# Rows of normalised v scaled during the last gate, output tiles held back for two norm waits, and two more weight slots in conv back

## The reference

```
for layer, mixer in ((0, pool), (1, conv), (2, sgu), (3, pool)):
    h = rmsnorm(x, g);  [branch..., z] = h @ W_in
    x = x + (mixer(branch) * silu(z)) @ W_out
sgu: vn = layernorm(v, ng, nb);  s = tril(W_s) @ vn + b   (chunks of 128 positions, 4 heads);  y = u * s
outputs: rmsnorm(x), pooling and conv histories,
         new_sgu_prompt = vn of the prompt's last 128 frames, new_sgu_sample = vn of the sample frames
```

## Time and profile before

| | us |
|---|---|
| three runs: lowest, median, highest | 3535.90, 3884.73, 4079.17 |
| the profiled execution | 3532.74 |
| its span on the slowest core (core 2) | 3531.3 |
| spans of the eight cores | 3508.8, 3529.5, 3531.3, 3507.0, 3502.7, 3525.1, 3499.4, 3521.7 |
| busy on core 2: PE, DVE, ACT, POOL | 3398.8, 2626.1, 1422.9, 759.2 |
| mean granted TensorE clock of core 2, share of full speed | 0.989 |

### The profile page before, as it was taken

One profiled execution on the slowest core, in us unless ns is written; L12 is line 12 of the kernel. 1 busy time (PEld: TensorE's weight loads), 2 busy tenths in 40 slices (PEclk: granted clock), 3 DMA queues, 4 the chain that ended last, 5 costly groups with the idle time before them and its releaser, 6 DMA issues.

```text
span 3531.3 us, 58242 instructions; the slowest of 8 cores (3499.4 to 3531.3 us)
## 1 busy us (share of the span) xinstructions
PE 3398.8 (96%) x17839; PEld 1709.5 (48%) x18112; DVE 2626.1 (74%) x4357; ACT 1422.9 (40%) x2202; POOL 759.2 (21%) x1388
## 2 busy tenths in 40 slices
PE   7999999999999999899999999999999899999997
PEld 3444444554555554444554444444455444444554
DVE  6879998986778877998765554555555788888886
ACT  3334443434455555655542333333233233333332
POOL 2323333312343342000011111111111221111220
PEclk9999999999999999999999999999999999999999
DMA  7798888578866668987886655774457843333343
GB/s 138 175 229 182 196 176 196 160 231 170 155 137 143 139 148 273 288 273 226 257 255 203 188 144 179 211 218 133 158 184 207 279 149 114 114 105 105 103 153 109
DMA packets 393329, 635.89 MB, mean 180 GB/s; under 512 B 170728, under 2 KB 234728, under 8 KB 385728
## 3 DMA queue, kind: packets, MB, share of 16 engines
q0 software_dynamic: 74960, 308.29, 34.3%
q1 hardware_dynamic: 318064, 323.86, 31.0%
HBM read 561.12 MB, written 197.23 MB: 215 GB/s over the span
## 4 chain that ended last, share of the span: by engine, by line
PE 85%; DMA 4%; DVE 4%; issue 3%; ACT 2%; SPq 1%; POOL 0%; DVEq 0%; ACTq 0%; POOLq 0%
PE ps L661 52%; PE ps L799 24%; PE ps L1502 6%; DMA arena<-xin 2%; PE ps L1233 1%; DVE arena L749 1%; DMA arena<-yd 1%; PE ps L861 1%; PE ps L1573 1%; DMA arena<-wq 1%; SPq L704 1%; DVE arena L742 0%; DMA arena<-wst 0%; DVE arena L958 0%; PE ps L1023 0%
## 5 line engine op out<-in xcount | busy, mean ns | idle before, releaser
L661 PE MATMUL ps<-arena 128*128 128x512 bf16 (+1 forms) x10195 | 2136.6, 363 | 24.3 <-DVE arena L958 4.8
L661 PEld LDWEIGHTS ps<-arena 128*128 128x128 bf16 x10368 | 1006.3, 98 | 1007.2 <-issue 33.6
L799 PE MATMUL ps<-arena 128*128 128x512 bf16 (+1 forms) x4546 | 951.6, 362 | 15.9 <-DVE arena L1412 5.7
L799 PEld LDWEIGHTS ps<-arena 128*128 128x128 bf16 x4608 | 450.6, 98 | 480.1 <-issue 21.8
L618 POOL DMA_DIRECT2D arena<-wq x435 | 231.3, 532 | 1398.3 <-PE ps L799 676.8
L958 DVE TENSOR_TENSOR arena<-arena 128x526 f32<-128x526 f32 (+6 forms) x720 | 472.5, 661 | 59.8 <-ACT arena L938 26.7
L712 ACT ACTIVATE arena<-arena 128x512 bf16<-128x512 f32 (+1 forms) x360 | 211.4, 591 | 647.8 <-DVE arena L803 601.4
L803 DVE TENSOR_TENSOR arena<-ps,arena 128x512 f32<-128x512 f32 (+1 forms) x288 | 184.4, 641 | 136.5 <-PE ps L799 120.7
L724 DVE TENSOR_TENSOR arena<-arena 128x512 f32<-128x512 bf16 (+3 forms) x258 | 165.6, 642 | 122.0 <-ACT arena L712 121.7
L979 ACT ACTIVATE arena<-ps 128x512 f32<-128x512 f32 (+1 forms) x288 | 161.7, 561 | 214.2 <-PE ps L661 206.0
L938 ACT ACTIVATE arena<-ps 128x512 f32<-128x512 f32 (+2 forms) x288 | 157.4, 547 | 207.8 <-PE ps L661 163.3
(11 more groups left out here) (97 smaller groups left out, 2543.6 us busy)
## 6 DMA issues: line engine op xcount, KB each, us to landing
arena<-wq POOLq DMA_DIRECT2D x435, 512.0 KB, 5.7
wq<-wst POOLq DMA_DIRECT2D x88, 512.0 KB, 8.0
xs<-arena SPq DMA_DIRECT2D x144, 256.0 KB, 7.0
arena<-xs SPq DMA_DIRECT2D x144, 256.0 KB, 6.7
arena<-wst POOLq DMA_DIRECT2D x64, 512.0 KB, 8.3
arena<-hd SPq DMA_DIRECT2D x26, 1024.0 KB, 7.8
arena<-xin SPq DMA_DIRECT2D x96, 256.0 KB, 7.9
yd<-arena SPq DMA_DIRECT2D x96, 256.0 KB, 5.4
```

Source lines behind the costliest of these rows:

```text
L661: r = e.matmul(P[:, 0:T], lhsT=W[:, k * 256 + base:k * 256 + base + 128], rhs=H[:, k * st:k * st + T], start=(k == 0), stop=(k == 7))
L799: r = e.matmul(P[:, 0:T], lhsT=W[:, k * 128:(k + 1) * 128], rhs=ym[k].ap(BF16)[:, 0:T], start=(k == 0), stop=(k == 15))
```

## The change

- `sgu_norm` no longer scales and stores the rows. It notes the chunk's f32 tile, its statistics and its output in `self.rows_out`.
- `row_steps` makes ten steps of it: for each quarter of the columns one tile with both parameter rows (ng and nb, one load of 512 KB, placed in pool vn), used by both chunks: three VectorE operations for each quarter and chunk (subtract-and-scale of 512 columns, multiply, add); then two stores. One step is written after each gate tile of group 8, from the third on.
- Pulls in the gating layer: group 0 pulls after quarters 1, 3, 5, 7, 9 and 12 of its 16 (counted from 0), the last group five times over its 12, and `pull(2)` after the last norm is `pull(3)`.
- Stage C may use two more slots, at R+116 KB and R+48 KB, and its CAP is 11. Its ym tiles of groups 1 to 8 are kept to 28 places, the upper of which end at R+48 KB.

```diff
-        self.slots = Pool(S, "slot", 4096, slots + A_ex + D_ex + C_ex + [R + 43 * kb, b + 45 * kb])
-        self.SL = {... "C": list(range(8)) + [26, 27, 28, 29], ...}
+        self.slots = Pool(S, "slot", 4096, slots + A_ex + D_ex + C_ex + [R + 43 * kb, b + 45 * kb] + [R + 116 * kb, R + 48 * kb])
+        self.SL = {... "C": list(range(8)) + [26, 27, 28, 29, 32, 33], ...}
-        self.CAP = {"A": 17, "B": 1, "C": 9, "D": 11, "E": 17}
+        self.CAP = {"A": 17, "B": 1, "C": 11, "D": 11, "E": 17}
...
-        o = self.ymp.tile(list(range(16 if g == 0 else 32)))
+        o = self.ymp.tile(list(range(16 if g == 0 else 28)))
...
-                    if (it % 2 == 1 if g == 0 else 6 * (it + 1) // (4 * nch) > 6 * it // (4 * nch)):
+                    if (it in (1, 3, 5, 7, 9, 12) if g == 0 else (5 if g == MIX else 6) * (it + 1) // (4 * nch) > (5 if g == MIX else 6) * it // (4 * nch)):
                         self.pull()
...
-            self.pull(2)
+            self.pull(3)
             hn = self.load_h(g + 1) if g + 1 < NG else None
             ym = []
+            steps = self.row_steps() if g == MIX else []
             for ct in range(16):
...
                 self.sgu_gate(g, ct, h, vns, bt, ym)
+                if steps and ct > 1:
+                    steps.pop(0)()
...
         if keep or samp:
-            S.add("dve", ... tensor_scalar of all 2048 columns ...)
+            self.rows_out.append((vr, sm, 1 if samp else 0))
+        return vn
+
+    def row_steps(self):
...
+        def step(q, vr, sm, t):
+            c = slice(q * 512, (q + 1) * 512)
+            if t.no not in loaded:
+                loaded.add(t.no)
+                src = self.sgrow[:, :, c].rearrange("i p c -> p i c")
+                S.add("sp", lambda e: e.dma_start(out=t.ap().rearrange("p (i c) -> p i c", i=2), in_=src), writes=[t], cost=0.45,
+                      nbytes=128 * 4096, dk=t)
+            S.add("dve", ... tensor_scalar(out=vr.ap()[:, c], ... op0=ALU.subtract, op1=ALU.mult) ...)
             for i, op in ((0, ALU.mult), (1, ALU.add)):
-                for q in range(4):
-                    t = self.tp.tile()
-                    S.add("sp", ... dma_start(out=t.ap(), in_=self.sgrow[i, :, q * 512:(q + 1) * 512]) ...)
-                    S.add("dve", ... tensor_tensor of quarter q ...)
-            S.add("sp", ... dma_start(out=dst, in_=vr.ap()) ...)
+                S.add("dve", ... tensor_tensor(out=vr.ap()[:, c], ..., in1=t.ap()[:, i * 512:(i + 1) * 512], op=op) ...)
...
+        for q in range(4):
+            t = self.vn.tile()
+            for vr, sm, i in self.rows_out:
+                out.append(lambda q=q, vr=vr, sm=sm, t=t: step(q, vr, sm, t))
+        for vr, sm, i in self.rows_out:
+            out.append(lambda vr=vr, i=i: store(vr, i))
+        return out
```

More of the change, by code:

```diff
@@ L527, in layout @@
         D_ex = offs(R + 102 * kb, 4096, 2) + offs(R + 38 * kb, 4096, 4)
-        self.slots = Pool(S, "slot", 4096, slots + A_ex + D_ex + C_ex + [R + 43 * kb, b + 45 * kb])
-        self.SL = {"A": list(range(20)), "B": [30, 31, 6, 7], "C": list(range(8)) + [26, 27, 28, 29], "D": list(range(8)) + [20, 21, 22, 23, 24, 25]}
+        self.slots = Pool(S, "slot", 4096, slots + A_ex + D_ex + C_ex + [R + 43 * kb, b + 45 * kb] + [R + 116 * kb, R + 48 * kb])
+        self.SL = {"A": list(range(20)), "B": [30, 31, 6, 7], "C": list(range(8)) + [26, 27, 28, 29, 32, 33], "D": list(range(8)) + [20, 21, 22, 23, 24, 25]}
         self.SL["E"] = self.SL["A"]
-        self.CAP = {"A": 17, "B": 1, "C": 9, "D": 11, "E": 17}
+        self.CAP = {"A": 17, "B": 1, "C": 11, "D": 11, "E": 17}
         self.zs = Pool(S, "zs", 2048, zs + C_zs + offs(R + 36 * kb, 2048, 8) + offs(R, 2048, 10))
@@ L1487, in sgu_layer @@
         h = self.h_next
+        self.rows_out = []
         for i, g in enumerate(range(NG)):
@@ L1544, in sgu_norm @@
         if keep or samp:
-            S.add("dve", lambda e: e.tensor_scalar(out=vr.ap(), in0=vr.ap(), scalar1=sm.ap()[:, 24:25], scalar2=sm.ap()[:, 27:28],
-                                                   op0=ALU.subtract, op1=ALU.mult),
-                  reads=[(sm, "r"), (sm, "mv")] + [(vr, q) for q in range(4)], writes=[(vr, q) for q in range(4)], cost=c_stt(2048))
-            for i, op in ((0, ALU.mult), (1, ALU.add)):
-                for q in range(4):
-                    t = self.tp.tile()
-                    src = self.sgrow[i, :, q * 512:(q + 1) * 512]
-                    S.add("sp", lambda e, t=t, src=src: e.dma_start(out=t.ap(), in_=src), writes=[t], cost=0.45, nbytes=128 * 2048, dk=t)
-                    S.add("dve", lambda e, t=t, q=q, op=op: e.tensor_tensor(
-                        out=vr.ap()[:, q * 512:(q + 1) * 512], in0=vr.ap()[:, q * 512:(q + 1) * 512], in1=t.ap(), op=op),
-                        reads=[t, (vr, q)], writes=[(vr, q)], cost=c_tt(512))
@@ L1556, in sgu_norm, with store @@
-            dst = self.o_sgu[1 if samp else 0]
-            S.add("sp", lambda e: e.dma_start(out=dst, in_=vr.ap()), reads=[(vr, q) for q in range(4)], writes=[("o_sgu", samp)],
-                  cost=0.45, nbytes=128 * 8192, dk=vr)
-        return vn
+            self.rows_out.append((vr, sm, 1 if samp else 0))
+        return vn
+    def row_steps(self):
+        S = self.S
+        out = []
+        def step(q, vr, sm, t):
[5 more added lines that the diff above has]
+                      nbytes=128 * 4096, dk=t)
+            S.add("dve", lambda e: e.tensor_scalar(out=vr.ap()[:, c], in0=vr.ap()[:, c], scalar1=sm.ap()[:, 24:25],
+                                                   scalar2=sm.ap()[:, 27:28], op0=ALU.subtract, op1=ALU.mult),
+                  reads=[(sm, "r"), (sm, "mv"), (vr, q)], writes=[(vr, q)], cost=0.41)
+            for i, op in ((0, ALU.mult), (1, ALU.add)):
+                S.add("dve", lambda e, i=i, op=op: e.tensor_tensor(out=vr.ap()[:, c], in0=vr.ap()[:, c],
+                                                                   in1=t.ap()[:, i * 512:(i + 1) * 512], op=op),
+                      reads=[t, (vr, q)], writes=[(vr, q)], cost=c_tt(512))
+        def store(vr, i):
+            S.add("sp", lambda e: e.dma_start(out=self.o_sgu[i], in_=vr.ap()), reads=[(vr, q) for q in range(4)],
+                  writes=[("o_sgu", i)], cost=0.45, nbytes=128 * 8192, dk=vr)
+        loaded = set()
+        for q in range(4):
[5 more added lines that the diff above has]
+        return out
```

## The result

The kernel after ran at 3509.23, 3512.24 and 3513.08 us, and once at 3989.87. Executions in which the cores of a die ran at a visibly lower clock, such as the last, are left out of every ratio here. The ratio to the kernel before is 0.9932 [0.9903, 0.9961], some 24 us of 3535, or 14 to 34. The profiled execution took 3509.23 us against 3532.74. The forecast was 3517: inside its range, 8 us too high.

The account below looks back on a forecast made before the run. TensorE, busy 3398.8 of 3531.3 us, bounds the kernel; only its 132 us of waits and their clock cost can be won. 3531.3 - 3.8 - 11.8 - 0 = 3515.7, plus 1.4 around the span: 3517 us, range 3506 to 3523 (0.56).

Parts of the forecast that it names:

- Part 3: Conv back: 18 fewer weight loads (9.4 MB) through two more slots and room for 11; taken as 0, bounds -8 and +24.
- the row on TensorE's own waits: Conv back: profile row showing TensorE waits for weights for 0.8 us in all; the ground for taking 0 there.
- The third of it that I allowed: Conv back: if 7.5% less traffic took a third of VectorE's 24.5 us wait for convolution rows, 8 us won.
- Part 1: First norm wait, group 0 of the gating layer: two output tiles cover the norm; gain 3.8 us, bounds 0 and 4.3.
- the second rival: First gate: the wait moves to its weights, landing 5 us late; Part 1 gains 0, loses 2; 3523 us, chance 0.10.
- Part 2: Last gate, group 8: row scaling leaves the last norm; excess 4.2 us instead of 16.0, gain 11.8, bounds 16.0 to 0.
- The 1.2 for the clock: Last gate: 1.2 us added for lower clock, about half of one seen loss, since waits come in small pieces.
- the fourth output tile: Before the last gate: four output tiles (10.4 us) instead of three cover a 5.1 us chain, so the 5.76 us wait goes.
- The first: Last gate: paced by VectorE, clock stays down, 16.8 us over seven tiles; 3529 us, chance 0.15.
- The third: Conv back: room goes into staying chunks, two slots stream; twelve loads late by 2 us each, 24 us; 3541, chance 0.12.
- The fourth: Last norm: planner still puts the steps' operations ahead of the last statistics, so no effect there; 3529 us, chance 0.03.

## Why the prediction was right and wrong

**The term that failed: Part 3 at 0.** I bounded conv back from -8 to +24 and took 0, "since the row on TensorE's own waits is the nearest". It measured -10.2 on the slowest core and -5.1 in the mean. That row was the wrong one to read: TensorE's waits for wq could give back 0.8 us. The row that showed what could be won was the next one, VectorE's 24.5 us for yd, which I named and set aside. The third of it that I allowed, 8 us, was near. The link that I had no proof for is that 18 loads fewer would shorten the stretch on the cores where other loads come late; the runs with 64 and 73 loads, the part alone and the added copies show it for the length of conv back. How much of it goes by way of yd is not shown: VectorE's waits for yd fell by 22 us, TensorE's for VectorE by 4.1. The second half of the miss is which core counts. Those 24.5 us were on the slowest core, and not on cores 0, 3, 4 and 6 (1 to 5 us). Such waits bear on the time because the late cores set it, and a mean over the cores hides them. Yet the 10.2 us are the size for this pair of executions, and in part luck: the time of the conv back part alone fell by 6 us, with an interval that reaches 0.

**Part 1** was 3.8 and is 5.1 on the slowest cores, 3.9 in the medians. The size holds in part by luck, since the pull alone, with the new conv back, is worth about 2 us. The argument that two output tiles cover the norm held: no wait, no lower clock, 3.7 us for 8.0. I treated it as apart from conv back, and it isn't: without that part group 0 is 1.9 us longer than before, by the second rival's wait for the gate's weights. In the change itself only 0.75 us of it came.

**Part 2** was 11.8 and is 11.7, the gate 46.8 for 46.8. That agreement is luck, and the step behind it is wrong. I had TensorE wait 3.6 us because a tile with a step needs 3.2 us of VectorE for 2.77 of TensorE, and took 0 for the parameter loads. It is the other way round. On cores 0, 2, 5 and 7 the same operations leave the gate at 42.7 us, with 0.7 us of waits of TensorE, so VectorE's added work costs nothing where the rows are there: the steps ran mostly before the norm of group 7's output and not beside it, since the planner had VectorE time there. TensorE's 3.95 us on core 3, and their like on cores 1 and 6, come only where VectorE waits for parameter rows, 3.9 us on core 3. The first two of TensorE's four waits stand right behind such a wait, the other two at the norm, where core 0 has a single one of 0.7. The 1.2 for the clock were not lost. And I credited the fourth output tile with part of the cover: the rows alone do it all.

**The rivals.** The first, a gate paced by VectorE with the clock down, did not come: four waits of 0.47 to 1.51 us within 17 us, and every 16 matmuls take 2.76 us at a clock of 1.00. The second failure mode of the Trainium skill's "TensorE: Matmul & The Clock Gate", by which that rival would have been the forecast, is thus not borne out by waits of this size. The kernel before does show it, for more than the two waits of the earlier trace rows: two others stand just ahead of them, core 2:

```profile
2754.50 1.46 PE L661 MATMUL ps<-arena 128*128 128x384 bf16 x8 [1.07 <-ACT arena L1591]
2756.69 1.46 PE L661 MATMUL ps<-arena 128*128 128x384 bf16 x8 [0.73 <-ACT arena L1591]
```

With 2.33 and 0.84 that is 4.97 us of waits within 8.2, and the 16 matmuls behind them take 5.28 us. The second rival is true of a kernel without the conv back part. The third, chunks that stay against slots that stream, came with CAP 10 in the old room and not in the change: with 11 and the new slots no core waits for a wq chunk in conv back (four wait 1.7 to 4.8 us for wst). The fourth is half true in its premise (the planner did move steps forward) and wrong in its price: ahead of the last statistics it put none that had to wait.

**What stays open.** Which of the two slots matters, and the pulls alone, were not tried. Why CAP 9 or 10 with the new slots brings 12 to 14, or 8.7 to 13.2, us of waits for L1412 on every core was not followed further. The stretch before conv back ended on the latest core at 1338 to 1349 us in different profiles (those with copies aside), and this scatter of 10 us is as large as the effect in question; the evidence for conv back is its own length on all cores, not the total. The two also offset each other: with the rows alone the cores that came at 1337.9, 1345.4 and 1348.0 us took 482.2, 474.6 and 468.8. So the last core reaches the first matmul of v at 1811.5 to 1820.1 us with the old conv back, at 1804.9 in the kernel after, but at 1810 to 1814 in the five other profiles with 55 loads and no copies. By these the part is worth 4 or 5 us on the core that comes last, and the profile of the kernel after was a lucky one.

## What to carry to other kernels

Where an engine with slack waits for a transfer, read that wait on the slowest core as something that may be won, not as slack: here fewer loads shortened the stretch, and the late cores got most of it. Where a forecast comes true on the slowest core, look at the other cores: here they showed that its reason was wrong. A change that frees a queue and one that moves a wait belong in one sum, since the second may only hold with the first. Where optional work sits on an engine ahead of work that others wait for, moving it out is what pays; more cover in front of it took the wait away and not the loss.

## What the runs showed of the hardware

- **One core of each neighbouring pair is late.** In every profile one of cores 0/1, 2/3, 4/5 and 6/7 reached conv back 3 to 32 us after its neighbour, and its span is 11.6 to 30.6 us longer; which one it was changed from run to run. Almost all long waits for yd are on the late ones. The spans of the kernel after show the pairs (the others are 3486.0 and 3507.7, 3500.6 and 3484.7, 3506.8 and 3484.8):

```profile
core 0: 3486.8 us, clock 0.993
core 1: 3506.8 us, clock 0.992
...
```

  The kernel's time is that of the late halves. What makes them late was not tested.
- **Small changes of traffic go with large changes of landing times.** Conv back moved 125 MB before and 252 GB/s x 464.3 us = 117 MB after, with the DMA engines busy for 0.85 and 0.81 of it. The median landing of the weight loads went from 7.5 to 6.2 us and the waits for yd from 24.5 to 2.5 on the slowest cores; the largest sum of these waits on any core went from 28.0 to 11.7. Twenty copies of 512 KB among the first pooling layer's loads left ten loads of 192 KB at 24.4 us (4.9 in the kernel after).
- **Row work on VectorE was free where its loads had landed.** The last gate takes 42.7 us on the four cores without a wait for parameter rows, and 43.3 to 46.8 on the four with 0.5 to 3.9 us of it.
- **The clock survived some waits.** 3.95 us of waits in four pieces within 17 us cost no clock, where 5.76 us in one piece cost 2.3 us, and 4.97 us in four pieces within 8.2 us cost 2.5 (5.28 for 2.76).
